# One decoder step on one core: in the dilated attention of the sample rows, the new key and value become rows of the third group's caches, and GpSimd stores the third group's rows before it waits for the second group's stores

## The reference, cut to what matters

```python
idx = n_past + jnp.arange(T)[:, None] - jnp.arange(n_slots + 1)[None, :] * dil
...
kg = kc[:, idx]          # kc, vc: the cache with the new row appended
vg = vc[:, idx]
s = jnp.einsum('bthe,btjhe->bthj', q, kg, preferred_element_type=F32) * DIL_HEAD_DIM ** -0.5 + bias_hj[None, None]
...
lse = jax.nn.logsumexp(s, axis=-1)
p = jnp.exp(s - lse[..., None])
o = jnp.einsum('bthj,btjhe->bthe', p, vg.astype(F32))
```

## Time and profile before

| What | Value |
|---|---|
| Median of 3 runs | 2618.98 us (2615.56 to 2620.22) |
| The profiled execution | 2619.3 us, span of its instructions 2617.8 us |
| PE matmuls busy | 2560.7 us, 98% of the span |
| DVE, ACT, POOL busy | 61%, 48%, 7% |
| Granted TensorE clock, mean | 0.993 |

### The profile page before, as it was taken

The page is one execution under the profiler, slowest core; times in us unless marked ns, Lnnn a source line. Parts: engine busy times, 40 slices in busy tenths (PEclk is TensorE's granted clock), DMA queues, the critical chain, the costliest instruction groups (busy, mean ns, idle before and its releaser), DMA issues. The chain is left out here.

```text
span 2617.8 us, 53803 instructions
## 1 busy us (share of the span) xinstructions
PE 2560.7 (98%) x20841; PEld 2474.6 (95%) x20841; DVE 1601.9 (61%) x2447; ACT 1252.2 (48%) x1951; POOL 195.1 (7%) x308
## 2 busy tenths in 40 slices
PE   8999999999999999999999999998999999999997
PEld 7988999999999999999999989987999999999997
DVE  5565656444555555545655566546777765777776
ACT  6555556334444444443444644345555555554553
POOL 1111111000111111100000002400000000000000
PEclk9999999999999999999999999999999999999998
DMA  8789788668888888866666747944566566666563
GB/s 245 224 255 299 242 267 248 183 187 223 236 235 230 231 233 227 224 181 190 174 177 201 204 126 231 308 146 122 166 184 179 158 187 192 186 177 179 162 186 107
DMA packets 855054, 530.97 MB, mean 203 GB/s; under 512 B 13961, under 2 KB 832065, under 8 KB 854135
## 3 DMA queue, kind: packets, MB, share of 16 engines
q1 hardware_dynamic: 822871, 440.20, 61.3%
q0 software_dynamic: 27312, 86.50, 9.5%
q10 hardware_dynamic: 4744, 2.48, 0.3%
HBM read 499.79 MB, written 33.29 MB: 204 GB/s over the span
## 5 line engine op out<-in xcount | busy, mean ns | idle before, releaser
L596 PE MATMUL bank<-h_hi,weights_hi 128*128 128x264 f32 x4624 | 1333.9, 288 | 16.1 <-DVE h_lo L2850 7.0
L569 DVE TENSOR_TENSOR weights_lo<-weights_raw,weights_hi 128x1024 fp32r<-128x1024 f32 x814 | 959.3, 1220 | 612.7 <-ACT weights_hi L561 612.5
L597 PE MATMUL bank<-h_lo,weights_hi 128*128 128x264 f32 x4624 | 1313.4, 284 | 0.0
L598 PE MATMUL bank<-h_hi,weights_lo 128*128 128x264 f32 x4624 | 1312.0, 284 | 0.0
L596 PEld LDWEIGHTS bank<-h_hi,weights_hi 128*128 128x128 f32 x4624 | 873.7, 189 | 42.0 <-issue 24.1
L561 ACT ACTIVATE weights_hi<-weights_raw 128x1024 fp32r<-128x1024 f32 x814 | 813.8, 1050 | 204.4 <-PE bank L598 193.3
L597 PEld LDWEIGHTS bank<-h_lo,weights_hi 128*128 128x128 f32 x4624 | 874.7, 189 | 2.1 <-issue 1.9
L598 PEld LDWEIGHTS bank<-h_hi,weights_lo 128*128 128x128 f32 x4624 | 869.9, 188 | 0.0
L596 PE MATMUL bank<-y_hi,weights_hi 128*128 128x264 f32 x1232 | 351.1, 285 | 5.0 <-DVE weights_lo L569 2.6
L598 PE MATMUL bank<-y_hi,weights_lo 128*128 128x264 f32 x1232 | 349.8, 284 | 0.0
L597 PE MATMUL bank<-y_lo,weights_hi 128*128 128x264 f32 x1232 | 348.3, 283 | 0.0
(11 more groups left out here) (415 smaller groups left out, 2189.2 us busy)
## 6 DMA issues: line engine op xcount, KB each, us to landing
weights_raw<-in_w_in SPq DMA_DIRECT2D x177, 1024.0 KB, 7.0
weights_raw<-in_w_up SPq DMA_DIRECT2D x88, 1024.0 KB, 5.7
weights_raw<-in_w_down SPq DMA_DIRECT2D x64, 704.0 KB, 5.0
gla_state_sample<-in_state_gla POOLq DMA_DIRECT2D x32, 512.0 KB, 8.9
out_gla_s<-gla_state_sample POOLq DMA_DIRECT2D x32, 512.0 KB, 6.1
weights_raw<-in_w_br_gla SPq DMA_DIRECT2D x16, 1024.0 KB, 6.1
weights_raw<-in_w_mix_out SPq DMA_DIRECT2D x16, 1024.0 KB, 6.2
weights_raw<-in_w_xkv SPq DMA_DIRECT2D x16, 1024.0 KB, 6.7
```

The lines of the kernel that those rows point to most:

```text
L569: nc.vector.tensor_tensor(w_lo[:, r, half], raw[:, r, half], w_hi[:, r, half].bitcast(F32), ALU.subtract).then_inc(lo_ready, 1)
L596: nc.tensor.matmul(out, wh, xh, start=first and n == 0, stop=False)
L597: nc.tensor.matmul(out, wh, xl, start=False, stop=False)
L598: mm = nc.tensor.matmul(out, wl, xh, start=False, stop=last and n == len(blocks) - 1)
```

## The change

New keys and values no longer have a path of their own. The three turned rows of a group become one transpose of a 128 x 24 tile, for which ACT copies the 8 sample columns of each product to a tile of their own, `qkvsT`. DVE copies 24 x 128 values. GpSimd stores all 24 rows (`d_qkv`). The new keys of all three groups are loaded as rows 64 to 66 of the third group's `kcache`, the new values as the same rows of its `vcache`, and the queries as the same rows of `qspread`. So the third group works on 67 rows (`ROWS`), the score columns are 323 in one piece, and the dot products, `v_new`, the diagonals and three matmuls are gone. The bias row needs no change, since its last three entries stand behind the 320. Of the three matmuls of `pst` two become transposes.

```diff
-        qkvs = at("qkv_sample", [NS, 3, 384], yt4 + 4608)
+        qkvs = at("qkv_sample", [3 * NS, 3, E], yt4 + 4608)
...
-        qkvT = at("qkv", [P, 9, T], R_Z)
+        qkvT = at("qkv", [P, 9, NP], R_Z)
+        qkvsT = at("qkv_of_samples", [P, 9, NS], R_Z + 9216)
...
-        V_DT = steps("vector_dil_tail", "qk2 pt1 m1 sc1 yl nw0 nw1 nw2 vn m2 sc2 sb sbn smx src sn dg0 dg1 dg2 yls")
+        V_DT = steps("vector_dil_tail", "qk2 pt1 m1 sc1 yl m2 sc2 sb smx src sn yls")
...
+        ROWS = (DSLOTS[0], DSLOTS[1], DSLOTS[2] + 3)
+        NEW = slice(DSLOTS[2], DSLOTS[2] + 3)
+
+        def new_row(kind, h):
+            return d_qkv[ds(h, 1), kind].rearrange("a g b e -> (a g) b e")
...
+            def v_new_load(h):
+                wait_here(sp, (dq_st, h * 48 + 48))
+                sp.dma_start(vcache[NEW, 2, :, :], new_row(2, h)).then_inc(v_in, 16)
...
+                        if j == 7:
+                            v_new_load(h - 1)
...
+            def dil_new(h, g):
+
+                wait_loop(pool, (V_DT if g == 2 else V_DIL).at(f"qk{g}", h))
+                pool.dma_start(d_qkv[ds(h, 1), :, g].rearrange("a v b e -> (a v) b e"), qkvs[:, g, :]).then_inc(dq_st, 16)
...
+                pool.dma_start(qspread[0:n, :, :].rearrange("p b e -> p (b e)"), row.to_broadcast([n, NS * E]))\
                     .then_inc(qb_in, 16)
+                if g == 2:
+                    pool.dma_start(qspread[NEW, :, :], new_row(0, h)).then_inc(qb_in, 16)
...
             def dil_tail(h):
-                dil_group(h, 2, G_DT("st2"))
-                wait_loop(pool, V_DT.at("sbn", h - 1))
+                dil_new(h, 2)
+                dil_stored(h, 1, G_DIL("st1"))
+                dil_group(h, 2)
+                dil_stored(h, 2, G_DT("st2"))
+                wait_loop(pool, V_DT.at("sb", h - 1))
...
-                    copy(qkvT[:, j, :], bank[p.outs[j]][:, 0:T]).then_inc(evac[p.outs[j]], 1)
+                    copy(qkvsT[:, j, :], bank[p.outs[j]][:, NP:T])
+                    copy(qkvT[:, j, :], bank[p.outs[j]][:, 0:NP]).then_inc(evac[p.outs[j]], 1)
...
+                    act.wait_ge(dq_st, h * 48 + 48)
+                    act.dma_start(kcache[NEW, :, :], new_row(1, h)).then_inc(k2_in, 16)
...
-                for v in range(3):
-                    mm = turn(bank[7][0:NS, v * P:v * P + P], qkvT[:, 3 * g + v, NP:T], P)
-                mm.then_inc(st(f"qs{g}"), 1)
+                turn(bank[7][0:3 * NS, 0:E], qkvsT[:, 3 * g:3 * g + 3, :].rearrange("p v b -> p (v b)"), P).then_inc(st(f"qs{g}"), 1)
...
-                    for g in range(3):
-                        n = DSLOTS[g]
-                        mm = nc.tensor.matmul(bank[7][0:n, NS * g:NS * g + NS], ssamp[:, g * P:g * P + n],
-                                              ident[0:NS, 0:NS], start=True, stop=True)
+                    nc.tensor.matmul(bank[7][:, 0:NS], ssamp[:, 0:P], ident[0:NS, 0:NS], start=True, stop=True)
+                    for g in (1, 2):
+                        n = ROWS[g]
+                        mm = turn(bank[7][0:n, NS * g:NS * g + NS], ssamp[:, g * P:g * P + n], NS)
...
-                    for g in range(3):
-                        nc.tensor.matmul(bank[3][:, E:E + NS], vnew[:, g, :], pdiag[:, g, :], start=g == 0, stop=False,
-                                         skip_group_check=True)
-                    nc.tensor.matmul(bank[3][:, E:E + NS], dom[:, :], dsel[:, :], start=False, stop=True,
-                                     skip_group_check=True).then_inc(P_DT("pvs"), 1)
+                    nc.tensor.matmul(bank[3][:, E:E + NS], dom[:, :], dsel[:, :], start=True, stop=True)\
+                        .then_inc(P_DT("pvs"), 1)
```

More of the change, by code:

```diff
@@ L735, in dil_last @@
                     v_load(7)
+                if j == 6:
+                    v_new_load(7)
             for j in range(DR):
@@ L906, in _, with dil_group @@
             pool.wait_ge(S_stored, 4 * 16)
-            def dil_group(h, g, step):
+            def dil_new(h, g):
+                wait_loop(pool, (V_DT if g == 2 else V_DIL).at(f"qk{g}", h))
+                pool.dma_start(d_qkv[ds(h, 1), :, g].rearrange("a v b e -> (a v) b e"), qkvs[:, g, :]).then_inc(dq_st, 16)
+            def dil_group(h, g):
                 new = A[f"dil{g + 1}_s"][0]
-                wait_loop(pool, (V_DT if g == 2 else V_DIL).at(f"qk{g}", h))
-                pool.dma_start(d_q[ds(h, 1), g].rearrange("a b e -> (a b) e"), qkvs[:, g, 0:E]).then_inc(dq_st, 16)
                 wait_loop(pool, (dq_st, h * 48 + (16 * g + 16)), V_DT.at("m2", h - 1) if g == 0
                           else V_DIL.at("m0", h) if g == 1 else V_DT.at("m1", h))
-                row = d_q[ds(h, 1), g].rearrange("a b e -> a (b e)")
-                pool.dma_start(qspread[:, :, :].rearrange("p b e -> p (b e)"), row.to_broadcast([P, NS * E]))\
+                row, n = d_qkv[ds(h, 1), 0, g].rearrange("a b e -> a (b e)"), DSLOTS[g]
+                pool.dma_start(qspread[0:n, :, :].rearrange("p b e -> p (b e)"), row.to_broadcast([n, NS * E]))\
                     .then_inc(qb_in, 16)
+                if g == 2:
+                    pool.dma_start(qspread[NEW, :, :], new_row(0, h)).then_inc(qb_in, 16)
                 wait_loop(pool, (A_DT if g == 2 else A_DIL).at(f"kv{g}", h))
@@ L924, in dil_group, with dil_stored @@
                                        kvtok[:, g, :, m, :]).then_inc(kv_st[g], 16)
-                pool.dma_start(new[:, 0, :, ds(h, 1), :].rearrange("b v a e -> b v (a e)"),
-                               qkvs[:, g, E:3 * E].rearrange("b (v e) -> b v e", e=E)).then_inc(qs_st[g], 16)
+                pool.dma_start(new[:, 0, :, ds(h, 1), :].rearrange("b v a e -> v b (a e)"),
+                               qkvs[NS:3 * NS, g, :]).then_inc(qs_st[g], 16)
+            def dil_stored(h, g, step):
                 for s, v in ((kv_st[g], h * (32 if g else 16) + (32 if g else 16)), (qs_st[g], h * 16 + 16)):
@@ L1241, in dil_tail @@
                     copy(apart[:, 0:2, :], bank[7][:, 0:16].rearrange("p (g b) -> p g b", b=NS)).then_inc(A_DT("ps0"), 1)
-                    copy(apart[0:64, 2, :], bank[7][0:64, 16:24]).then_inc(A_DT("ps1"), 1)
+                    copy(apart[0:ROWS[2], 2, :], bank[7][0:ROWS[2], 16:24]).then_inc(A_DT("ps1"), 1)
                 if k == 7:
@@ L2419, in dil_qk @@
                 dve.wait_ge(*saved)
-                nc.vector.tensor_copy(qkvs[:, g, :], bank[7][0:NS, 0:384]).then_inc(st(f"qk{g}"), 1)
+                nc.vector.tensor_copy(qkvs[:, g, :], bank[7][0:3 * NS, 0:E]).then_inc(st(f"qk{g}"), 1)
             def dil_cached(h, g, st):
-                n = DSLOTS[g]
-                dve.wait_ge(qb_in, h * 48 + (16 * g + 16))
-                dve.wait_ge(*((k2_in, h * 16 + 16) if g == 2 else (k_in, h * 32 + (16 * g + 16))))
+                n = ROWS[g]
+                dve.wait_ge(qb_in, h * 64 + (16, 32, 64)[g])
+                dve.wait_ge(*((k2_in, h * 32 + 32) if g == 2 else (k_in, h * 32 + (16 * g + 16))))
                 nc.vector.tensor_tensor(kcache[0:n, :, :], kcache[0:n, :, :], qspread[0:n, :, :], ALU.mult)\
@@ L2470, in dil_tail @@
                                             ALU.subtract).then_inc(V_DT("yl"), 1)
[L2471 to L2474, removed]
-                        nc.vector.tensor_tensor_reduce(out=qk_junk[:, :], in0=qkvs[:, g, 0:E], in1=qkvs[:, g, E:2 * E],
-                                                       scale=1.0, scalar=0.0, op0=ALU.mult, op1=ALU.add,
-                                                       accum_out=snew[:, g:g + 1]).then_inc(V_DT(f"nw{g}"), 1)
-                    dve.wait_ge(*P_DT.at("pvs", h - 1))
-                    nc.vector.tensor_copy(vnew[:, :, :], qkvs[:, :, 2 * E:3 * E]).then_inc(V_DT("vn"), 1)
                 if k == 3:
```

36 lines of the change are left out of this document (12 added, 24 removed).

## The result

| | before | changed |
|---|---|---|
| First measurement, median | 2618.12 us (5 runs, 2615.56 to 2620.22) | 2607.06 us (5 runs, 2602.46 to 2609.73) |
| Ratio, 95% interval | | 0.995 (0.9939 to 0.996) |
| Second measurement, median | 2619.26 us (17 runs) | 2601.70 us (6 runs, 2599.11 to 2607.71) |
| Ratio, 95% interval | | 0.9937 (0.9924 to 0.9949) |
| Profiled execution, its span | 2619.3 us, 2617.8 us | 2605.87 us, 2604.4 us |

The forecast was 2603.1 us in a range of 2600.0 to 2608.0. Both medians lie in the range, on either side of the forecast; the two intervals overlap between 0.9939 and 0.9949, a saving of 13 to 16 us. The two profiled executions are 2617.8 - 2604.4 = 13.4 us apart.

The account below looks back on a forecast made before the run. PE's start-to-start steps were taken to bound the dilated stage. Savings of 5.3 + 6.8 + 1.6 + 2.2 = 15.9 us, off a profiled 2619.3 us, gave an expected median of 2603.1 us, range 2600.0 to 2608.0.

Parts of the forecast that it names:

- The bound: Dilated stage, 590 to 1152 us: time is the sum of PE's start-to-start steps; other engines' gains are worth nothing.
- Part 1: Turns of the sample rows: nine small transposes a head become three, 0.11 us each, saving 5.3 us for eight heads.
- Part 2: New values: three matmuls' six instructions and a long first step go, 0.85 us a head, 6.8 us; lower end 6.1.
- Part 3: Probabilities back to slots: six instructions become four, 0.20 us a head, 1.6 us in all, ends 0.8 and 2.4.
- Part 4: Tail steps 5 and 7, 67 rows instead of 64: 0.28 us a head, 2.2 us; ends -0.2 and 2.6.
- none of them for a sample row: Dilated stage before the change: PE's single wait of 0.2 us was read as not for a sample row, cache or tile.
- PE's waits in the stretch still a fraction of a microsecond: Sign expected in the profile after: PE's waits in the dilated stage stay under a microsecond.
- rival 2: Steps saved but PE waits elsewhere, for tiles or normalised scores; 2607 to 2619 us; 6 in 100.
- as a block: Stages after the dilated one, paced by PE or by chains starting from it, were to move up together.
- The costs called nothing: Off PE: ACT's 72 small copies, at most 12.0 us, a DMA issue a head and new store waits were to cost nothing.
- SyncE's new wait: Ahead of product 7's tile load: perhaps 2 us later; PE feels nothing until SP is about 17 us late.
- rival 3: Slower: SP's wait for the third group's store over 17 us; saving gone at 19, 2643 us at 22; 3 in 100.

Follow-up runs that it names:

- two extra turns: Changed kernel with two more transposes a group, of key and value columns, into columns nobody reads; dilated stage 5.2 us longer than in the changed kernel.
- three extra matmuls: Changed kernel with three float32 matmuls of 8 weight rows again ahead of tail step 8's last one, output unread; dilated stage 6.6 us longer than changed.
- 64 rows: Changed kernel with 64 instead of 67 rows in the third group, new key and value left out; dilated stage 2.4 us longer than changed.
- two more float32 instructions: Changed kernel with three float32 matmuls in tail step 6 again, the third with 67 columns; dilated stage 1.9 us longer than changed.
- last head first: Changed kernel with the last head's tail step 8 ahead of the weight-tile split on ScalarE and VectorE; stage 1.5 us shorter than changed, median 2602.32 us.
- the stores waited for first: Changed kernel with GpSimd waiting for the second group's stores ahead of the third group's store; stage 0.0 us different from changed, one run 2601.94 us.
- SyncE's wait for the scores: Changed kernel with SyncE waiting until VectorE summed the third group's scores before loading new value rows; stage 62.5 us longer than changed, one run 2663.15 us.

## Why the prediction came out right, step by step

**The bound.** The sum of PE's steps sets this stage, and PE's waits stayed at one entry. Shown by the ruler: two extra turns, three extra matmuls, 64 rows and two more float32 instructions each cost what the steps add up to, within 0.2 us.

**Part 1**, 5.3 us forecast, 5.2 measured by the two extra turns. **Part 2**, 6.8 forecast, 7.6 measured. The mis-sized piece is what follows the three matmuls. The last matmul's two instructions take from 703.74, in the earlier trace rows, to 703.98, the start of the next, 0.24 us, and I took that as their own price; after the change the same pair takes 0.14, from 702.03 to 702.17. **Part 3**, 1.6 forecast, 2.5 read from the steps. I had taken 0.20 us a head between ends of 0.10 and 0.30 and it was 0.31, of which 0.23 come from the transposes. **Part 4**, 2.2 forecast, 2.8 read from the steps. Step 5 gained 0.24 instead of 0.13 us, with the matmul behind it counted, and step 7 only 0.11 instead of 0.15 (1.54 us before, 1.43 now). The run with 64 rows, 2.4 us, gives a little less, since in it step 6 gains 0.02 to 0.03 us a head.

**What the sum left out.** 5.2 + 7.6 + 2.5 + 2.8 = 18.1 us, and the stage gained 16.8. Of the missing 1.3 us 1.0 is in the last head. I had read the 0.2 us in the earlier trace rows as "none of them for a sample row", and it was a wait for the last head's sample rows that the three matmuls nearly covered: shorten PE's way to it by 0.95 us and it grows to 1.2. This is the step that failed, "PE's waits in the stretch still a fraction of a microsecond", and "last head first" shows its place. It is rival 2 on a small scale, at a place that the rival did not name. The other 0.3 us are spread over the steps of the products in pieces of about 0.01 us, and what makes them is open.

**Luck in the sum.** Three of the four parts came out above their upper ends of 6.8, 2.4 and 2.6 us. Together the parts were 2.2 us more than forecast, and the wait and the small pieces took 1.3 of it back. That 15.9 us stands so near to 16.8 is in part owed to this.

**The other stages** did not move "as a block", or not only. They scatter by up to 5.7 us from one profile to the next with setup apart, whatever the kernel, and the first median stood 4.0 us above the forecast and the second 1.4 below. In the first pair of profiles the stage's 16.8 us, less 2.7 behind it and 0.6 of setup, leave the 13.4 us of the whole, to a tenth. The interval of the first measurement ends at a saving of 16.0 us, under the stage's 16.8, and that of the second holds it. That a lost clock is part of the scatter is shown by the windows. That it is all of it, and that it alone parted the two medians, is not shown.

**The costs called nothing** were nothing: 12.7 us of copies on ScalarE, the third group's store, and SyncE's new wait of 60.4 us in eight heads. The reason given for SyncE was incomplete. I counted when PE needs the late tile, and not that ScalarE's queue holds the sample scores behind it, where PE has under 1 us to spare. At 7 us of lateness nothing is seen, and at 16 the kernel is slower than before by 45 us (one run each), so rival 3's thresholds of 17 and 19 us were too generous.

## What to carry to other kernels

Where PE never waits, price an edit by the steps from start to start of its instructions, and look for matmuls whose rows or columns have another form than their neighbours': giving the odd one the common form, though larger, gained 0.3 us a head here. Before calling a small wait nothing, ask what covers it, since whatever shortens the way to it lengthens the wait. And when a load is late, follow the whole queue behind the engine that stands at it, not only the tile.

## What the runs showed of the hardware

Going from full weights to 8 rows makes the first step 0.21 us (702.77 to 702.98) where 0.12 is usual, and going from 128 rows to 64 makes it 0.20. A float32 matmul of full 128 x 128 weights and 8 columns takes 0.24 us to the next start directly behind the three 8-row matmuls, in the kernel before and again with three matmuls more, and 0.14 behind a product. Whether the change of form makes these 0.1 us, or that the matmuls ahead are short, no run separates. The long first steps are in line with the Trainium skill, page TensorEngine Tiling, section Key Properties, which has a change of mode drain the array and gives no time for it. The other rule of that page that was weighed, up to twice the speed for a contraction of at most 64 rows, is not borne out in this kernel, where the array is not split into tiles of 64 rows that work side by side: with 64 rows the stage is 2.4 us longer than with 67.

A wait of PE can cost more than its length. In SyncE's wait for the scores PE waited 43.9 us, and half clock near their ends and behind them took another 18 us. The 2.1 us for which PE waits until 1296.7 us in the changed kernel were followed by half clock in both profiles of the changed kernel and not in the one with the stores waited for first.
